# Two transformer blocks on one core: four modulation panels taken during the branch projections, residual sums and norm factors placed ahead of weight halves

## The reference, cut to what matters

```python
mod = c_act @ w_ada + b_ada               # shift_t, scale_t, gate_t, shift_f, scale_f, gate_f
...
merged = gate_a * (o_a @ w_branch_a) + gate_b * (o_b @ w_branch_b)
mix = merged @ w_o
x = layernorm(ALPHA * x + gate_t * mix, ln1_g, ln1_b)
h = x * (1.0 + scale_f) + shift_f
u = causal_dwconv(h @ w_up, conv_ffn) + b_conv_ffn
u_gate, u_val = split(u)
ffn = (silu(u_gate) * u_val) @ w_down
x = layernorm(ALPHA * x + gate_f * ffn, ln2_g, ln2_b)
```

## Time and profile before

| | |
|---|---|
| median of 3 runs (lowest, highest) | 1036.68 us (1034.71, 1036.95) |
| the profiled execution's own time | 1037.48 us |
| its span in the trace | 1035.7 us |
| TensorE busy, VectorE busy, ScalarE busy | 955.3, 702.7, 547.3 us |
| mean granted TensorE clock | 0.972 of 2.4 GHz |
| read from HBM | 194.43 MB |

### The profile page before, as it was taken

The page is one execution under the profiler, slowest core; times in us unless marked ns, Lnnn a source line. Parts: engine busy times, 40 slices in busy tenths (PEclk is TensorE's granted clock), DMA queues, the critical chain, the costliest instruction groups (busy, mean ns, idle before and its releaser), DMA issues.

```text
span 1035.7 us, 19911 instructions
## 1 busy us (share of the span) xinstructions
PE 955.3 (92%) x8438; PEld 903.5 (87%) x8438; DVE 702.7 (68%) x1112; ACT 547.3 (53%) x829; POOL 27.0 (3%) x71
## 2 busy tenths in 40 slices
PE   4699999969999999799899999989998699999995
PEld 1489999869999999699699998978998499999994
DVE  2659937677777665888774543566568778888744
ACT  2658232654544435756736334466764466766434
POOL 2100000000000000400100000000000000000000
PEclk9899999989999999899999999999999799999997
DMA  9834656548888887257424336543457545656921
GB/s 333 283 102 148 246 197 211 196 131 272 278 271 277 286 274 265 82 182 250 130 91 145 124 129 147 184 144 122 140 188 248 177 130 178 196 185 199 326 91 41
DMA packets 57400, 196.78 MB, mean 190 GB/s; under 512 B 6096, under 2 KB 10592, under 8 KB 57056
## 3 DMA queue, kind: packets, MB, share of 16 engines
q1 hardware_dynamic: 51840, 187.72, 54.2%
q10 hardware_dynamic: 5216, 7.53, 2.8%
q0 software_dynamic: 256, 0.26, 0.1%
HBM read 194.43 MB, written 1.06 MB: 189 GB/s over the span
## 4 chain that ended last, share of the span: by engine, by line
PE 76%; DVE 13%; ACT 5%; DMA 2%; issue 2%; ACTq 0%; SPq 0%; DVEq 0%
PE panel_banks L399 65%; DVE w_lo L1460 3%; DVE mix_work L1802 3%; DMA raw<-in_panels 2%; PE work_banks L768 2%; ACT w_hi L946 2%; DVE raw L1493 1%; PE work_banks L596 1%; PE work_banks L697 1%; PE work_banks L739 1%; PE work_banks L556 1%; PE work_banks L529 1%; PE work_banks L851 1%; PE work_banks L796 1%; ACT gla_work L984 0%
## 5 line engine op out<-in xcount | busy, mean ns | idle before, releaser
L399 PE MATMUL panel_banks<-act_hi,w_hi 128*128 128x256 f32 (+1 forms) x1600 | 462.0, 289 | 25.9 <-DVE w_lo L1460 10.1
L399 PE MATMUL panel_banks<-act_lo,w_hi 128*128 128x256 f32 (+1 forms) x1600 | 454.0, 284 | 0.0
L399 PE MATMUL panel_banks<-act_hi,w_lo 128*128 128x256 f32 (+1 forms) x1600 | 453.5, 283 | 0.0
L1460 DVE TENSOR_TENSOR w_lo<-raw,w_hi 128x1024 fp32r<-128x1024 f32 x260 | 315.5, 1222 | 141.6 <-ACT w_hi L946 140.9
L946 ACT ACTIVATE w_hi<-raw 128x1024 fp32r<-128x1024 f32 x260 | 272.3, 1055 | 164.0 <-PE panel_banks L399 121.7
L399 PEld LDWEIGHTS panel_banks<-act_hi,w_hi 128*128 128x128 f32 x1600 | 303.8, 190 | 38.5 <-issue 20.7
L399 PEld LDWEIGHTS panel_banks<-act_lo,w_hi 128*128 128x128 f32 x1600 | 304.4, 190 | 1.9 <-issue 0.5
L399 PEld LDWEIGHTS panel_banks<-act_hi,w_lo 128*128 128x128 f32 x1600 | 303.9, 190 | 1.6
L399 PE MATMUL panel_banks<-hidden_hi,w_hi 128*128 128x256 f32 x352 | 98.6, 280 | 2.4 <-ACT hidden_hi L1165 2.4
L399 PE MATMUL panel_banks<-hidden_hi,w_lo 128*128 128x256 f32 x352 | 98.4, 279 | 0.0
L399 PE MATMUL panel_banks<-hidden_lo,w_hi 128*128 128x256 f32 x352 | 98.2, 279 | 0.0
(11 more groups left out here) (268 smaller groups left out, 974.7 us busy)
## 6 DMA issues: line engine op xcount, KB each, us to landing
raw<-in_panels SPq DMA_DIRECT2D x356, 512.0 KB, 5.1
mix_work<-delta_rows ACTq DMA_DIRECT2D x2, 1024.0 KB, 11.9
x_t<-in_x ACTq DMA_DIRECT2D x1, 1024.0 KB, 9.4
gla_work<-in_ctx_x ACTq DMA_DIRECT2D x1, 1024.0 KB, 14.5
mix_work<-in_rel_bias ACTq DMA_DIRECT2D x1, 1024.0 KB, 10.2
out_x<-ffn_work SPq DMA_DIRECT2D x4, 256.0 KB, 2.5
mix_work<-in_rel_bias ACTq DMA_DIRECT2D x1, 768.0 KB, 14.9
c_wide<-in_c_rows ACTq DMA_DIRECT2D x1, 512.0 KB, 4.0
```

Source lines behind the costliest of these rows:

```text
L399: ins = pe.matmul(out_, a, b, start=start and p == 0, stop=stop and p == 2, skip_group_check=True)
L1460: dve.tensor_tensor(wlo[:, v_ % PARTS, :], raw[:, u % RAW, :], whi[:, v_ % PARTS, :].bitcast(F32), ALU.subtract)\
```

## The change

Five edits, and no arithmetic is added, removed or done on other numbers.

1. `LAYERS`: the four A panels that stood between the mix panels now follow a2, a3, b0 and b1. The mix panels follow each other without a gap in the stream.
2. VectorE sums them inside `tend`, each right after the second low half of the S panel ahead of it; the `accumulate()` calls in the merge loop, after it and in the mix loop are gone.
3. The five small steps that finish shift_f, scale_f and the layer norm's gains stand ahead of the mix loop instead of ahead of the centring.
4. In the mix loop `residual` comes after one weight half instead of after two (and, for the first two, after the A panel). The second half of the second `up` panel is made inside the layer norm, behind its folds (`between`; in the second layer norm that half has long been made, so nothing moves there).
5. Ahead of `qkv`, ScalarE takes the norm factor first, then one half, and the other half after the `h3` tiles; VectorE takes both halves after the `h3` tiles. Ahead of the first SwiGLU VectorE takes one half instead of two ahead of the scaled tiles.

```diff
-          ("branch_a", "S", 4), ("branch_b", "S", 4), ("mix", "SA", 4), ("up", "S", 22),
+          ("branch_a", "S", 2), ("branch_a_rest", "SA", 2), ("branch_b", "SA", 2),
+          ("branch_b_rest", "S", 2), ("mix", "S", 4), ("up", "S", 22),
...
-            upper_parts(j + 1)
             act.wait_ge(S("norm_sum"), 4)
             factor(rs[:, 0:T], MB[:, 0, 0:T], D, 0, "norm_factor")
+            upper_half(2 * j + 2)
             for r in range(4):
                 act.wait_ge(S("x_new"), 5 + r)
...
                     act.activation(hhi[:, k, :], h3[:, k, :], ACT.Copy).then_inc(S("h3_hi"), 1)
+            upper_parts(j + 1)
...
-            lower_parts(j + 1)
+            lower_half(2 * j + 2)
             dve.wait_ge(S("x_new"), 4)
             dve.wait_ge(S("norm_factor"), 3)
...
-            lower_parts(j + 1)
             dve.wait_ge(S("panel_evacuated"), first["qkv"][1])
...
                         lower_tile(k, h3[:, k, :], "h3")
+            lower_parts(j + 1)
...
                     lower_half(2 * j + taken[0] + PARTS)
                     taken[0] += 1
+                    if taken[0] in (50, 52, 54, 56):
+                        accumulate()
...
-                if i == 2:
-                    accumulate()
                 merge(i)
...
             lower_parts(j + 1)
-            accumulate()
+            dve.wait_ge(S("accumulated"), 72)
+            then(dve.tensor_tensor(mod2[:, 24:40], mod2[:, 24:40], col("b_ada_2", 24, 16), ALU.add))
...
             for i in range(4):
-                if i == 3:
-                    residual(first["mix"][1], i)
-                lower_parts(j + 2)
-                if i < 2:
-                    accumulate()
+                lower_half(2 * j + 4)
+                residual(first["mix"][1], i)
                 if i < 3:
-                    residual(first["mix"][1], i)
+                    lower_parts(j + 2)
                 j += 1
...
                     fold("ln_squares", 4 * count + r - 3, "folded")
+                lower_half(between)
                 dve.wait_ge(S("ln_centred"), 4 * count)
```

More of the change, by code:

```diff
@@ L1992, in _, with layer_norm @@
             lower_parts(j + 1)
-            accumulate()
-            for i in range(4):
-                if i == 3:
-                    residual(first["mix"][1], i)
-                lower_parts(j + 2)
-                if i < 2:
-                    accumulate()
+            dve.wait_ge(S("accumulated"), 72)
+            then(dve.tensor_tensor(mod2[:, 24:40], mod2[:, 24:40], col("b_ada_2", 24, 16), ALU.add))
+            then(dve.tensor_scalar(sc_a[:, 1, :], mod2[:, 32:40], 1.0, None, ALU.add))
+            dve.tensor_tensor(gcol[:], sc_a[:, 1, :], col("ln1_g_2", 0, 8), ALU.mult)
+            then(dve.tensor_tensor(sc_a[:, 0, :], sc_a[:, 1, :], col("ln1_b_2", 0, 8), ALU.mult))
+            then(dve.tensor_tensor(sc_a[:, 0, :], sc_a[:, 0, :], mod2[:, 24:32], ALU.add))
+            for i in range(4):
+                lower_half(2 * j + 4)
+                residual(first["mix"][1], i)
                 if i < 3:
-                    residual(first["mix"][1], i)
+                    lower_parts(j + 2)
                 j += 1
-            def layer_norm(count):
+            def layer_norm(count, between):
                 dve.wait_ge(S("ln_in"), 4 * count)
@@ L2014, in layer_norm @@
                     fold("ln_squares", 4 * count + r - 3, "folded")
+                lower_half(between)
                 dve.wait_ge(S("ln_centred"), 4 * count)
                 dve.wait_ge(S("ln_factor"), count)
-            dve.wait_ge(S("accumulated"), 72)
-            then(dve.tensor_tensor(mod2[:, 24:40], mod2[:, 24:40], col("b_ada_2", 24, 16), ALU.add))
-            then(dve.tensor_scalar(sc_a[:, 1, :], mod2[:, 32:40], 1.0, None, ALU.add))
-            dve.tensor_tensor(gcol[:], sc_a[:, 1, :], col("ln1_g_2", 0, 8), ALU.mult)
-            then(dve.tensor_tensor(sc_a[:, 0, :], sc_a[:, 1, :], col("ln1_b_2", 0, 8), ALU.mult))
-            then(dve.tensor_tensor(sc_a[:, 0, :], sc_a[:, 0, :], mod2[:, 24:32], ALU.add))
-            layer_norm(1)
+            layer_norm(1, 2 * j + 3)
             staggered(lambda k: dve.scalar_tensor_tensor(h2[:, k, :], y3[:, k, :], gcol[:, k:k + 1], rs[:, T:2 * T],
@@ L2068, in _ @@
                 residual(first["down"][1], r)
-            layer_norm(2)
+            layer_norm(2, 2 * j - 1)
             for k in range(KT):
```

## The result

| | before | changed |
|---|---|---|
| median (lowest, highest) | 1036.82 us (1034.71, 1038.37), 4 runs | 1027.72 us (1027.22, 1029.73), 4 runs |
| ratio, with its 95% interval | | 0.9912 (0.9894 to 0.9930) |
| profiled execution, its span | 1037.48, 1035.7 us | 1028.15, 1026.4 us |
| mean granted TensorE clock | 0.972 | 0.977 |
| HBM read | 194.43 MB | 194.43 MB |

The change makes the kernel 9.1 us faster by these runs; 1028.7 us was predicted, within 1026.0 to 1032.0.

A forecast was written before the change was run, and what follows sets the result against it. TensorE, busy 92% of the span, was taken as the bound, with only its waits to win: 4.06 + 1.77 + 1.68 + 0.43 = 7.94 us off the 1036.68 us median gives 1028.7 us, range 1026.0 to 1032.0.

The forecast's parts named there:

- Step 1: Mix: with the A panels gone, TensorE's three waits of 0.49, 2.44 and 1.13 us go, -4.06 us.
- Step 2: Branches: taking in the A panels and their sums on VectorE costs TensorE 0, bounded by +1 us.
- No TensorE wait between a3 and m0: Branches, expected sign: TensorE never waits for `w_lo` from a3 to m0.
- a wait of 1 us or more at b2: Branches: a TensorE wait this long at b1 or b2 would make the prediction wrong.
- The branches starve: Rival, branches: late halves make TensorE wait 1 us each at b2 and b3, 1030.7 us; chance 0.10.
- Slower: Rival, branches: VectorE becomes the bound, none of the sums' 9.2 us is hidden, 1037.9 us; chance 0.03.
- Step 3: First layer norm: centring starts right behind the mean, at 815.85 instead of 817.62 us, -1.77 us.
- Step 4: Ahead of `qkv`: the norm factor starts sooner, so VectorE scales from 415.83 instead of 417.51 us, -1.68 us.
- The bounds of -0.8 and -2.5: Ahead of `qkv`: range in us for the gain, depending on when TensorE's clock returns to 2.4 GHz.
- Step 5: Ahead of the first SwiGLU: VectorE starts at 221.17 instead of 221.60 us, -0.43 us.
- The panels themselves are at their floor: Panels on TensorE: each takes 5.65 us, so only time in which TensorE stands still can be won.
- the sums run at full clock: Rival, layer norm: the clock holds at 2.4 GHz, up to 1.5 us more is won, 1027.2 us; chance 0.15.

The follow-up runs named there:

- the run with spread panels: The changed kernel with the four A panels behind the 7th gate panel, a0, a2 and b0 instead of a2, a3, b0 and b1: 1031.70 us, ratio 0.9942.
- ten runs: All runs of the unaltered changed kernel, from both its series: median 1029.3 us, 7.5 us faster than the kernel before.
- the first series: The first four runs of the unaltered changed kernel, against the kernel before: 1027.72 us, ratio 0.9912.
- the padding: The changed kernel with unread products of ones by ones filling five TensorE gaps: 1026.98 us; with fewer products, cut to size, 1023.55 us.

## Why the prediction was right, and where not

*Step 1, mix, right.* Three waits, 4.06 us, forecast and gone, by the A panels alone. From b3's to m3's evacuation it is 806.25 - 783.07 = 23.18 us instead of 28.34 (m3 stood at 812.52): 5.16 less, not 4.06. Half of the difference is how a wait is read. The idle time runs from the modelled end of a product, 0.28 us behind its start, while the next could have started after 0.12. Each wait costs 0.16 us more than its number: three waits, 0.5 us. Another 0.3 us is no part of the change: in its mix 65 products ran at the faster spacing, 4.4 ns less each, in that of before none. The last 0.3 is not explained.

*Step 2, the branches: the term that failed.* "No TensorE wait between a3 and m0", 0 with a bound of +1, was 1.40 us in the profiled execution, and 0.81 to 1.49 in seven others with this order (an eighth, the single run with the SwiGLU edit undone, had 0.23). The prediction had named a wait of 1 us or more at b2 as a sign of being wrong, and here it was. Two things under it were off. A half was taken to arrive every 1.34 us, from the 390 GB/s of the earlier trace rows; that was the best 8 us of the stage. The window of the changed kernel where the ring is fullest:

```profile
760.00:770.00 10.00, 10.00 (x86) 9.88 (x84) 7.82 (x9) 5.12 (x7) 0.00 (x0) 1.00 0.97 344
```

At a DMA share of 0.97 it moved 344 GB/s, 1.52 us a half. VectorE's three idle times of 0.46, 1.11 and 1.06 us come from this; I had counted about 1 us in all. The delay arose at the halves of b1: they were done at 765.50 us, which is 768.1 in the prediction's times (the changed kernel is 2.6 us ahead at this point), and 766.9 was predicted. Everything behind them kept its distance. The Trainium skill, "DMA: Bandwidth & Descriptors", section Bandwidth, gives a limit of about 358 GB/s for a core, and by it the prediction had worked out that the half would be late. The trace agrees with it here, within 4%; the 390 GB/s of the earlier trace rows and 385 GB/s from 764 to 772 us in the run with spread panels were above it, so it is no hard cap for this core, but it was the better figure for a stage. The second is the order on VectorE: the margin was as thin as 0.3 us only because `ya` (2.28 us) stood ahead of the half, and moving it removes the wait. "The branches starve" was thus half right: one wait instead of two, for VectorE's order as much as for the ring. "Slower" did not come: of the 9.2 us of sums only the 1.4 us at b2 reached TensorE.

*Step 3, layer norm, right:* 1.80 us for 1.77.

*Step 4, `qkv`: the mechanism was right, the size was not.* 1.71 us at the first product (1.68 forecast), but 1.0 on average 76 us later (0.8 in the pair of before and changed), since more work falls into the half-speed stretch. The bounds of -0.8 and -2.5 named this cause; the value taken between them ignored it.

*Step 5, SwiGLU, right* as far as it can be told: about 0.46 for 0.43, with a spread as large.

*What the sum did not have.* Ahead of the first panel TensorE waited 7.19 us in before and 6.08 in the changed kernel; the code there is the same, and traces of the other variants have 5.7 to 6.1 or 7.2. Ahead of the sums over q and k it waited 3.71 and 2.12. Over all traces this wait is 3.3 to 3.7 us where the faster spacing held until 470 us or longer, and 2.0 to 2.3 otherwise: what TensorE's rate wins in those 12 panels is for the most part lost in that wait. So of the 9.3 us between the two spans 4.5 are mix, 1.8 the layer norm, 0.8 `qkv`, 0.7 SwiGLU and 1.1 the chance at the start, less 1.6 for b2: 7.3 us in all. Of the last 2, about 1.1 are half-speed stretches outside the `qkv` panels that cost less (over the whole span their cost is the same, 17.5 and 17.4 us, because the one in `qkv` costs 1.0 more), and 0.3 the faster spacing in mix; the rest is spread thinly.

*How much of the hit is luck.* The edits alone make 6.2 us in this pair, and 6.6 with the means of all traces (4.5, 1.8, 1.0 and 0.5, less 1.2 for b2); 7.94 was forecast. The two misses, 1.2 to 1.6 us at b2 and 0.7 to 0.9 at `qkv`, go the same way, and only the 0.5 us that mix gave beyond its waits goes against them. The medians say 7.5 us (ten runs) and 9.1 (the first series, 7.3 to 11.0 by its interval). That the forecast lies so near to them is partly luck: in the pair of traces the start, the half-speed stretches and the spacing made up the difference, and none of them is a term of the sum.

*The floor.* "The panels themselves are at their floor", 5.65 us each, was not so: with the 113.4 ns spacing one panel of the changed kernel's mix took 5.44 us (evacuated at 788.65 and 794.09 us in ScalarE's timeline).

*The rival "the sums run at full clock"* did not come by this change: the eight sums took 3.65 us. It came with the padding, 1.2 to 1.4 us from the last mean sum to `up`.

## What to carry to other kernels

Work that other engines could do at any time (sums for a later stage, weight halves of later panels) belongs where no one waits for its engine, and the place has to be checked for the instruction that then comes last: here one gate product of 2.3 us on VectorE in front of an urgent half gave back 1 us of 4. A TensorE wait costs more than its length where the clock falls behind it, so a shorter wait may bring less than it saves, and filling it with products that nobody reads, cut to end before the data comes, brought more than any single edit here (5.8 us by the medians). When the runs of one kernel scatter by more than an edit is worth, price the edit by waits that repeat between traces.

## What the runs showed of the hardware

- At a granted clock of 1.00 the panels' products (128x128 by 128x256) start every 113.4 or every 117.8 ns, for tens of microseconds at a time, and in part differently from execution to execution.
- Standstills of 2.8 to 6.2 us ahead of the sums and panels in question were followed by the 1.2 GHz level in every trace without padding. With padding that left 0.6 us or less of them the clock stayed at 2.4 GHz ahead of `qkv` and through the layer norm in all five padded traces; with 0.86 us left ahead of the first SwiGLU product the lower level came back behind it in two of four.
- A float32 product of 128x128 by 128x256 leaves two records and took 0.45 us at full speed.
- With three to six halves on the way the landing came 6.6 us after issue (median; 5.3 to 8.2), with one or two 3.8 us (3.6 to 4.8), as these rows of the `raw` tile have it, for 755 to 772 us and 700 to 740 us of the changed kernel:

```profile
DMA to landing us min/median/max: 5.3/6.6/8.2
```

```profile
DMA to landing us min/median/max: 3.6/3.8/4.8
```
